# RWKV-7 scan of a hybrid diffusion backbone: key and b operands as one 128-column weight, U stacked on the values, transposes by TensorE's transpose

## What is computed

```python
def wkv_scan(r, w, k, v, a, b, S0, reverse):
    def step(S, inp):
        rt, wt, kt, vt, at, bt = inp
        sa = jnp.einsum('bhvk,bhk->bhv', S, at)
        S = S * wt[:, :, None, :] + sa[..., None] * bt[:, :, None, :] + vt[..., None] * kt[:, :, None, :]
        return S, jnp.einsum('bhvk,bhk->bhv', S, rt)
    S_fin, ys = lax.scan(step, S0, xs, reverse=reverse)
# rwkv_mix: for d in range(2): wkv_scan(rh, decay, kd, vh, -kk, kk * a, S0[d], reverse=(d == 1))
#           the context runs first from a zero state, the latent tokens start from its final state
```

## Time and profile before

| | us |
|---|---|
| three timed executions | 2356.69, 2350.64, 2346.11 (median 2350.64) |
| profiled execution, its own time | 2349.85 |
| its span in the profile | 2348.2 |
| mean granted TensorE clock | 0.954 of full |
| PE / DVE / ACT / POOL busy, share of the span | 90% / 31% / 21% / 12% |
| scan of layer 0 | about 415 to 622 |
| scan of layer 1 | about 1619 to 1820 |

### The profile page before, as it was taken

How to read it: one execution, slowest core, us unless ns; L and a number is a source line. 1 busy time by engine, 2 the same in 40 slices (tenths; PEclk the granted TensorE clock), 3 DMA queues, 4 the chain that set the end, 5 groups by cost and what they waited for, 6 DMA issues and landing times. The chain is left out here.

```text
span 2348.2 us, 53901 instructions
## 1 busy us (share of the span) xinstructions
PE 2101.7 (90%) x23898; PEld 1349.7 (57%) x23898; DVE 720.6 (31%) x1768; ACT 487.9 (21%) x1120; POOL 274.7 (12%) x463
## 2 busy tenths in 40 slices
PE   6999899899899999999999789898999899987784
PEld 2454443889644444446556465554898788754442
DVE  1033334777431011310100032546676311200002
ACT  2123312333220000301111132323332301110011
POOL 0000000443100001101111100001343000011111
PEclk8999999899999999999999989998899999998996
DMA  7148716000121212448999821110000344799993
GB/s 287 61 154 344 305 65 226 3 4 4 56 90 54 108 54 108 181 161 328 398 383 395 306 90 51 69 50 1 4 4 4 146 159 188 274 378 397 395 406 122
DMA packets 55828, 399.91 MB, mean 170 GB/s; under 512 B 6672, under 2 KB 22928, under 8 KB 33648
## 3 DMA queue, kind: packets, MB, share of 16 engines
q1 hardware_dynamic: 43440, 361.94, 39.9%
q0 software_dynamic: 8576, 23.08, 2.6%
q10 hardware_dynamic: 3648, 12.45, 1.7%
HBM read 365.47 MB, written 31.98 MB: 169 GB/s over the span
## 5 line engine op out<-in xcount | busy, mean ns | idle before, releaser
L494 PE MATMUL ps<-H,memory 128*128 128x512 f32 (+2 forms) x1728 | 615.1, 512 | 11.6 <-DMA memory<-in_w_in 9.7
L494 PEld LDWEIGHTS ps<-H,memory 128*128 128x128 f32 (+1 forms) x1728 | 327.5, 190 | 286.5 <-issue 251.6
L731 PE MATMUL ps<-memory 64*64 64x32 f32 (+2 forms) x10112 | 329.0, 229 | 33.6 <-DVE memory L1624 10.1
L994 PE MATMUL ps<-memory 128*32 128x256 f32 x5120 | 298.8, 395 | 49.2 <-DMA memory<-in_eu 47.7
L731 PEld LDWEIGHTS ps<-memory 64*64 64x64 f32 x10112 | 316.4, 142 | 43.3 <-issue 21.3
L494 PE MATMUL ps<-memory 128*128 128x512 f32 (+3 forms) x928 | 319.2, 495 | 6.2 <-issue 3.0
L994 PEld LDWEIGHTS ps<-memory 128*32 128x32 f32 x5120 | 184.8, 114 | 160.0 <-issue 71.0
L494 PEld LDWEIGHTS ps<-memory 128*128 128x128 f32 (+1 forms) x928 | 173.8, 188 | 143.6 <-issue 127.3
L1019 PE MATMUL ps<-memory 128*32 128x256 f32 x2560 | 144.8, 380 | 5.0 <-ACT memory L1342 3.8
L1914 POOL TENSOR_TENSOR memory<-memory,cons 128x256 f32<-128x256 f32 x160 | 117.9, 752 | 122.5 <-DVE memory L1596 78.7
L1019 PEld LDWEIGHTS ps<-memory 128*32 128x32 f32 x2560 | 79.6, 110 | 59.9 <-ACT memory L1342 10.1
(11 more groups left out here) (251 smaller groups left out, 1804.9 us busy)
## 6 DMA issues: line engine op xcount, KB each, us to landing
memory<-in_eg SPq DMA_DIRECT2D x32, 2048.0 KB, 17.2
memory<-in_eu SPq DMA_DIRECT2D x32, 2048.0 KB, 23.0
memory<-in_ed SPq DMA_DIRECT2D x32, 2048.0 KB, 23.4
memory<-in_w_ada SPq DMA_DIRECT2D x24, 2048.0 KB, 9.5
memory<-in_w_in SPq DMA_DIRECT2D x20, 2048.0 KB, 7.6
expert_rows<-memory SPq DMA_DIRECT2D x4, 3456.0 KB, 23.7
memory<-in_w_out SPq DMA_DIRECT2D x4, 2048.0 KB, 7.8
memory<-expert_rows ACTq DMA_DIRECT2D x19, 384.0 KB, 10.4
```

Source lines behind the costliest of these rows:

```text
L494: ins = mm(ps[0:M, bank, 0:w], lhs(k), rhs(k), start=(k == 0), stop=(k == n - 1))
L731: ins = mm(out[cols, j], lhs[rows, j, :], rhs[rows, j], start=(n == 0), stop=(n == len(terms) - 1))
L994: ins = mm(out_.rearrange("p (x n) -> p x n", x=2), XGT[:, k, g * GROUP:g * GROUP + GROUP], sets[b][:, 0:2, k * 512 + c * P:k * 512 + c * ...
```

## The change

Only the scan stage differs. Layout: `BB[d]` holds, for every j, bE2 and bKk side by side as one 64x128 weight (`bE2` on side d, `bKk` on side 1-d). `UV[d]` holds on 128 partitions U (side d) and the values (side 1-d); `BK` and `GR` are their 128-row partners (turned b and k; masked products with the queries).
- `grams`: 8 products per direction with a 64x128 weight and 128 moving columns (64 where no queries are needed), in place of 16 (8) with 64x64 weights. They write one bank per head.
- `turns` and `values`: `pe.transpose` of 64x128 blocks, 16 and 8 per step, in place of 32 and 16 products.
- `readout`: 16 products of S with the queries and 16 with 128-row operands, in place of 48. `update`: 16 with 128 rows, in place of 32.
- `correct` is two passes, `correct_values` and `correct_state`, and the second waits for the first's semaphore.
- Masks on VectorE: two operations of 512 columns per direction (the second on 64 partitions) in place of three of 256.
- ScalarE: U and values are copied as 64 partitions x 512 columns in place of 128 x 256; `pick`, a new copy, gathers both directions' values.
- Order: couple, correct_values, grams(0), correct_state, grams(1), solve, then the levels. `join` of level 0 waits for the U copies of both directions. `turns` for both directions moves from level 0 to level 1, `readout` to level 2, `update` of both directions between the joins of level 3, `values` behind the last `grow`. `read` on VectorE moves from levels 1 and 2 to levels 2 and 3.

```diff
+        BK = [[pairs(piece(2)) for d in range(2)] for p in range(2)]
+        GR = [[pairs(piece(2)) for d in range(2)] for p in range(2)]
+        UV = [pairs(piece(2)) for d in range(2)]
+        BB = [pairs(piece(2)) for d in range(2)]
...
                 def grams(k, d):
-                    heads("grams", (ps[:, 4 * d + 1, 0:256 * wide].rearrange("p (x j n) -> p j x n", x=wide, n=CH),
-                                    (ONCE["bKk"][d], ER[p][d][:, 0:wide].rearrange("p x j n -> p j x n"), 0, 0)))
+                    for j in range(RJ):
+                        for h in both:
+                            ins = mm(ps[:, bank(d, h), 128 * j:128 * j + CH * wide], BB[d][side(h), j], ER[p][d][side(h), 0:wide, j],
+                                     start=True, stop=True)
...
                 def turns(k, d):
-                    heads(None, (part(d, 0, 0), (ONCE["bE2"][d], eye, 0, 0)))
-                    heads("turns", (part(d, 0, 1), (ONCE["bKk"][d], eye, 0, 0)))
+                    for j in range(RJ):
+                        for h in both:
+                            ins = pe.transpose(ps[:, bank(d, h), CH * j:CH * j + CH], BB[d][side(h), j], eye[side(h), :])
...
+                def correct_values(k):
+                    for j, d, h in problems:
+                        ins = mm(part(d, 3, 0)[side(h ^ d), j], GAK[side(1 - d), j, h], UV[d][side(1 - d), j, h],
+                                 start=(j == 0), stop=False)
+                    ins.then_inc(sem("values"), 1)
+                def correct_state(k):
+                    pe.wait_ge(sem("values"), corrected(N))
...
+                def readout(k):
+                    for j, d, h in problems:
+                        mm(part(d, 1, 0)[side(h), j], ONCE["S"][d][side(h), j], ER[p][d][side(h), 1, j], start=(j == 0), stop=False)
+                    for j, d, h in problems:
+                        ins = mm(part(d, 1, 0)[side(h), j], UV[d][:, j, h], GR[p][d][:, j, h], start=False, stop=(j == RJ - 1))
+                def update(k):
+                    for j, d, h in problems:
+                        ins = mm(part(d, 0, 0)[side(h), j], BK[p][d][:, j, h], UV[d][:, j, h], start=True, stop=True)
...
                 def join(k, n, d):
                     if n == 0 and k:
-                        pe.wait_ge(sem("u_copied"), nth(N - 1, d))
+                        pe.wait_ge(sem("u_copied"), nth(N - 1, 1))
...
+                        if n == 1 and more:
+                            for d in both:
+                                turns(k, d)
+                        if n == 2 and k and streams(l, k - 1):
+                            readout(k - 1)
+                        if n == 3 and k:
+                            update(k - 1)
                         join(k, n, 1)
...
                 def solve(k):      # ScalarE
-                        act.copy(flat(ONCE["U"][d]), part(d, 3, 1)).then_inc(sem("u_copied"), 1)
+                        rows = side(d)
+                        act.copy(by_head(UV[d])[rows], quarters(rows, slice(bank(0, 3), bank(1, 3) + 1), 1)[:, ::-1 if d else 1]).then_inc(sem("u_copied"), 1)
...
                 def masks(k, d):   # VectorE
-                        tt(TWICE["Grb"][p][d], half(d, 0, 1), over_pairs(con_(f"incl{d}")), ALU.mult)
-                        tt(TWICE["Grk"][p][d], half(d, 1, 1), over_pairs(con_(f"incl{d}")), ALU.mult)
+                        tt(by_head(GR[p][d]), made[:, :, :, 1], over_heads(con_(f"incl{d}")), ALU.mult)
...
-                        if k and n in (1, 2):
-                            read(k - 1, n - 1)
+                        if k and n in (2, 3):
+                            read(k - 1, n - 2)
```

212 lines of the change are left out of this document (121 added, 91 removed).

## The result

The changed kernel takes 2404.8 us (median of 4 runs, 2400.5 to 2418.0) against 2351.3 for the kernel before on the same chip: a ratio of 1.024, 95% interval 1.019 to 1.029, slower. The forecast was 2364 with a range up to 2393. The sign was right, the size was not. The profiled run took 2408.7 us.

What follows compares the result with a forecast made beforehand. The prediction took each scan step as a loop through TensorE and VectorE: 2349.85 us, -15 from shorter steps, +28 from half clock, gave 2363, or 2364 with 0.8 for the median; range 2325 to 2393.

Steps and rivals of the forecast that it cites:

- TensorE's work: Scan, streaming step: fewer or cheaper turns, readout, update, values and grams save 3.4 us of TensorE time per step.
- the 1.2 us set aside for changes of mode: Scan step: TensorE's array changes tile shape about 12 times at 0.1 us each, 1.2 us a step.
- the rival with column halves one after the other: Readout and update: 64-column weights load in turn, each costs 0.95 us more; +24 us, 2388 us, chance 0.13.
- The walk: Scan step followed through both engines from the coupling: streaming 23.7 against 23.94 us, without output 20.7 against 21.56; -15 us together.
- The rival in which TensorE stays the bound: Scan: no idle time appears and TensorE's savings pay, -50 us at most, -40 likely; 2310 us, chance 0.10.
- the stall behind the U copies: Level 0's join waits 1.5 us for both U copies, hidden behind VectorE, showing only beyond 1.1 us more.
- The amount of half clock: Scan: TensorE's clock falls after level 0 and at the step's end, 8 us per step in 14 steps.
- Its price: Scan: half clock costs 0.25 us per us, 14 x 8 x 0.25 = +28 us.
- Last steps and tails at 0: Ends of both scans: first and last steps and tails change by 0 us.
- Signs: Scan: streaming steps 25 to 26.5 us, clock 0.8 to 0.9, TensorE busy under 20, join waiting 1.5, readout near 1.9.
- The clock holds: Scan: the dense parts carry the clock, so only the -15 us remain; 2336 us, chance 0.20.
- Transposes don't hold the clock: Scan, after level 1: a third clock fall per step, +14 us; 2378 us, chance 0.07.

Runs made afterwards that it cites:

- reordered kernel: The changed kernel with the earlier order at a step's head (both corrections, first Gram group, solve, second Gram group, first addition): 2384.6 us, ratio 1.015.
- filled: The changed kernel with thrown-away products in all idle stretches of TensorE (ahead of level 0, in later levels, at the step's end): 2365.4 us, ratio 1.005.
- the filled kernel before: The kernel before with thrown-away products at levels 1 and 2 of steps without readout and level 3 of a layer's first step: 2349.7 us, ratio 0.999.
- the versions with fewer falls: The reordered kernel with turns ahead of level 1's first join and steps without readout filled, fully or more lightly: 2352.2 and 2351.6 us, both ratio 1.000.
- the products: The changed kernel with turns of keys and values as float32 products with the identity instead of true transposes: 2455.2 us, ratio 1.045.
- filling the end: Thrown-away products at each step's end: on the changed kernel 2421.3 us; on the reordered kernel with steps without readout filled 2402.8 us.

## Why the prediction was wrong in size

**TensorE's work: right.** TensorE's timeline of the reordered kernel, at full clock, has the turns, the two halves of the readout, the update and the values:

```profile
524.29 0.71 PE L800 MATMUL ps<-cons,memory 64*128 64x64 f32 x16
...
527.02 1.15 PE L844 MATMUL ps<-memory 64*64 64x64 f32 x32
528.10 1.15 PE L846 MATMUL ps<-memory 128*64 128x64 f32 x32
...
531.37 1.15 PE L858 MATMUL ps<-memory 128*64 128x64 f32 x32
...
536.31 0.46 PE L778 MATMUL ps<-cons,memory 64*128 64x64 f32 x8
```

By its rows: turns 0.71 us, predicted 0.75; streaming grams 1.16 per direction, predicted 0.90; readout 2 x 1.15, predicted 1.9; update 1.15, predicted 0.95 and its share of mode changes; values 0.46, predicted 0.4. The saving is 1.25 + 0.30 + 0.56 + 0.81 + 0.52 = 3.4 us a step, the 3.4 of the sum. That the sum is met this closely is in part luck: grams, readout and update are each longer than their price, and the 1.2 us set aside for changes of mode, which no row shows by themselves, cover it. The 32 products with 128 rows take 1.08 us from start to start, 34 ns each and not 58, so the rival with column halves one after the other falls.

**The walk: right but for the stall.** No step of the changed kernel had the clock full throughout, so the walk is seen in the other versions: a streaming step was put at 23.7 and measured 23.6, 24.3 and 24.6 (filled) and 23.6 with a short fall (reordered); one without output at 20.7 and measured 20.84 and 20.68, both with thrown-away products in them. TensorE's 3.4 us come back as under 1. The rival in which TensorE stays the bound falls with it. The part that failed is the stall behind the U copies: foretold as 1.5 us, hidden and showing only beyond 1.1 more, it was 1.35 long and made VectorE wait 0.45 to 0.61 at level 0, so in the changed kernel VectorE doesn't set level 0. It cost 0.7 us in the step of 24.38 and 1.3 in a step at half clock.

**The amount of half clock: the step that failed.** "I expect 8 us of half clock per step" was 10.2 in the full streaming steps and all of the step, 31 us, in layer 1's three without readout: 237 us in fourteen steps against the 112 that were summed. The larger part is layer 1's, 165 us. I had placed falls after each sparse stretch and let the clock recover in between. In layer 1 it did not recover for 133 us (1630.1 to 1763.2). Why it did not stays open. The kernel before enters that scan at half clock too, for its first 11 us, and falls again 18 us in (0.79 in a window of the earlier trace rows); I read that row for its price and not for what would follow if the recovery failed.

**Its price: near by average, low for a fall in the middle.** Taken at 0.25 us per us; measured on equal instructions 0.37 to 0.43 for a fall in the middle of a step, and 0.30 where the whole step is at half. Over both scans the steps are 48.9 us longer, and 15 should have been gained, so 64 us are to be explained. The walk stood for a full clock, but for the two first steps, which were left as before with their 25 us of half clock; so 212 us of half clock came on top, 0.30 each, and the stall's cost is in that. At the predicted price the missing 100 us of half clock are 25 of the 46 us by which the span's growth was missed; price and stall are 11, the ends of the scans 12.5, all else -2.7. The value of 0.09 in the earlier trace rows, which pulled my choice down, was misread: the step of 24.56 us has no readout (673 matmuls) and the one it was compared with has (769). The same error counts that step among nine full streaming ones; there are eight. Against its own form at full clock, in the filled kernel before, it gives 0.25.

**Last steps and tails at 0: wrong by 12.5 us.** TensorE's timeline of the end of layer 1's scan, after the change and before it:

```profile
1867.69 0.69 PE L809 MATMUL ps<-memory 64*64 64x64 f32 x32 [1.37 <-ACT memory L1297]
...
1870.11 1.14 PE L830 MATMUL ps<-memory 64*64 64x64 f32 x32 [0.94 <-ACT memory L1302]
1872.60 1.98 PE L844 MATMUL ps<-memory 64*64 64x64 f32 x32 [1.35 <-ACT memory L1308]
1874.50 1.75 PE L846 MATMUL ps<-memory 128*64 128x64 f32 x32
```

```profile
1812.80 1.33 PE L731 MATMUL ps<-memory 64*64 64x64 f32 x64 [0.59 <-DVE memory L1640]
1815.08 0.69 PE L731 MATMUL ps<-memory 64*64 64x64 f32 x32 [0.95 <-ACT memory L1230]
1816.22 3.02 PE L731 MATMUL ps<-memory 64*64 64x64 f32 x96 [0.45 <-ACT memory L1235]
```

Where no next step covers them, all waits lie bare: 1.37 for the copies of the values, which before were turned a step earlier, and 1.35 for the U copies against 0.45. And the readout runs at half clock (3.7 us against 3.0). From the first of these to the end it is 8.6 us against 6.4. The rest of the 7.4 us lies ahead of them: before, a last step has no turns and values to make and is over in 21.1 us (1791.72 to 1812.80), after, it takes 26.4 (1841.30 to 1867.69), in which the long fall lies. In the versions with fewer falls the ends still take 29 to 34 us.

**Signs.** Of those that were to show the forecast right, the wait of `join` (1.35 us), the clock of layer 0 (0.80) and the readout (2.2 us) came. Streaming steps took 24.4 to 28.0 and not 25 to 26.5, the clock of layer 1 was 0.59, and TensorE was busy 21 to 25 us of a streaming step and not under 20.

**Rivals.** "The clock holds", 2336, stands refuted by the clock. Its size isn't tested, since no version holds the clock; the shortest ends of the scans in any version (60.7 us for both, against 57.3 before) would still take 3 us of its gain. "Transposes don't hold the clock" gets no support from the products.

**What stays open.** What starts a fall is shown in part: a wait of 1.35 to 1.65 us, 6 to 9 us into the step, goes with the long fall in most streaming steps that have one. Taking the wait away, by order, by turns or by filling, left most full streaming steps of layer 0 without a fall in their middle in eight kernels (in the one with all waits filled, in half of them), and filling the end, which lets TensorE arrive earlier, brought it back in one and lengthened it in another. Against the wait as the whole cause stand the step of 24.38 us, which has it and no long fall, and the filled steps of both layers that fell without it. Those, the steps of the reordered kernel that stay at half clock with no such wait, and the way a layer enters its scan at half clock, are not explained by these runs. The Trainium skill's page TensorE: Matmul & The Clock Gate, Part 1 (how oscillation bites in real kernels), describes a kernel in which TensorE waits for a DMA in every round of its loop and starts each round at the lower clock. The step of 27.37 us agrees in that half clock goes with a wait; its twin of 23.61 and the step of 24.38 show that here it doesn't come in every round.

## What to carry to other kernels

Work taken from an engine that isn't alone in setting a loop turns into waits, and on TensorE a wait of 1.35 to 1.65 us in a stretch of small products can go with a fall of the clock that costs 2.9 to 3.8 us a step: put real work (here the turns) into the wait that appears before counting any gain. Don't fill idle time at random: a slow head hidden behind another engine can go with a faster step, and filling the end of the step took one kernel from 2359 to 2403 us. Price the ends of a pipelined loop apart from its steps, since there every new wait is bare.

## What the runs showed of the hardware that I had not expected

- The same instructions in neighbouring steps take 23.61 or 27.37 us, by where the clock's fall lies and how long it is (3.4 us at the head, 10.2 in the middle). Each form repeats: five steps in a row at 27.2 to 27.3 with the end filled, four at 23.6 to 23.8 in the reordered kernel.
- A row of steps of small products can stay at half clock: three steps of 30.9 us in a row at 0.50, with TensorE busy 29.2 of 30.9 us by its rows.
- A transpose is one instruction where a float32 product is two in the trace: 14.1 us for the turns as 224 transposes, 45.9 as 448 products.
- Thrown-away products that kept TensorE busy for 98% of a step by its rows (30.25 of 30.93 us) did not hold its clock: it was 0.65.
